# A delta rule's triangular inverse: the transposed inverse is kept and updated by products instead of being made by transposes

## The reference

```
g = jnp.cumsum(g, axis=-1)
decay = jnp.exp(jnp.where(tri_incl, g[..., :, None] - g[..., None, :], -jnp.inf))
k_beta = k * beta[..., None]
lower = jnp.where(tri_strict, jnp.einsum('bhncd,bhnsd->bhncs', k_beta, k) * decay, 0.0)
rhs = jnp.concatenate([v * beta[..., None], k_beta * jnp.exp(g)[..., None]], axis=-1)
sol = lax.linalg.triangular_solve(lower, rhs, left_side=True, lower=True, unit_diagonal=True)
...
v_new = ui - jnp.einsum('bhck,bhkv->bhcv', wi, state)
o = jnp.einsum('bhck,bhkv->bhcv', qd, state) + jnp.einsum('bhcs,bhsv->bhcv', qki, v_new)
state = state * jnp.exp(gl)[..., None, None] + jnp.einsum('bhck,bhcv->bhkv', kt, v_new)
```

## Time and profile before

| | us |
|---|---|
| median of 3 runs | 2580.62 |
| lowest and highest run | 2569.69, 2582.98 |
| span of the profiled execution | 2578.2 |
| TensorE busy in it | 2375.5 |
| VectorE busy in it | 1323.9 |
| ScalarE busy in it | 788.4 |
| GpSimd busy in it | 494.4 |

### The profile page before, as it was taken

One profiled execution on the slowest core, in us unless ns is written; L12 is line 12 of the kernel. 1 busy time (PEld: TensorE's weight loads), 2 busy tenths in 40 slices (PEclk: granted clock), 3 DMA queues, 4 the chain that ended last, 5 costly groups with the idle time before them and its releaser, 6 DMA issues.

```text
span 2578.2 us, 33292 instructions
## 1 busy us (share of the span) xinstructions
PE 2375.5 (92%) x13498; PEld 1918.1 (74%) x13498; DVE 1323.9 (51%) x1688; ACT 788.4 (31%) x1106; POOL 494.4 (19%) x350
## 2 busy tenths in 40 slices
PE   6867699999989999999999998999997987999997
PEld 5745577777877777788888876888885665888885
DVE  3799755664654243454445336444425675444423
ACT  4213322221542321333223224223223353233221
POOL 0799333313031332010000002000002013000001
PEclk8978898899989999999999997999997987999998
DMA  3221111111210111242223321222321101222321
GB/s 137 68 82 49 49 38 38 38 42 46 74 34 25 35 41 58 70 155 90 98 98 102 101 100 66 83 97 98 114 92 55 58 25 66 82 96 93 118 90 44
DMA packets 54899, 189.64 MB, mean 74 GB/s; under 512 B 6144, under 2 KB 6400, under 8 KB 54784
## 3 DMA queue, kind: packets, MB, share of 16 engines
q1 hardware_dynamic: 51904, 182.75, 20.9%
q10 hardware_dynamic: 2880, 5.24, 0.5%
HBM read 178.53 MB, written 9.44 MB: 73 GB/s over the span
## 4 chain that ended last, share of the span: by engine, by line
PE 75%; DVE 13%; issue 9%; ACT 1%; DMA 1%; SPq 0%; POOL 0%; DVEq 0%; ACTq 0%; POOLq 0%
PE pg L571 61%; PE pC L755 3%; DVE sacc L1606 2%; DVE cacc L1496 2%; PE pB L746 2%; PE pB L745 1%; PE pB L602 1%; DVE w_lo L1453 1%; DVE x L1932 1%; PE pC L609 1%; DVE a_lo L1478 1%; PE pB L609 1%; PE pC L746 1%; DVE hb L1928 1%; ACT w_hi L1027 1%
## 5 line engine op out<-in xcount | busy, mean ns | idle before, releaser
L571 PE MATMUL pg<-a_hi,w_hi 128*128 128x512 f32 x1904 | 780.4, 410 | 72.6 <-DVE a_lo L1478 36.9
L571 PE MATMUL pg<-a_hi,w_lo 128*128 128x512 f32 x1904 | 774.4, 407 | 0.0
L571 PE MATMUL pg<-a_lo,w_hi 128*128 128x512 f32 x1904 | 770.0, 404 | 0.0
L1453 DVE TENSOR_TENSOR w_lo<-w_raw,w_hi 128x1024 fp32r<-128x1024 f32 (+3 forms) x299 | 394.4, 1319 | 436.7 <-ACT w_hi L1027 436.7
L1027 ACT ACTIVATE w_hi<-w_raw 128x1024 fp32r<-128x1024 f32 (+3 forms) x299 | 329.7, 1103 | 700.4 <-PE pg L571 675.5
L571 PEld LDWEIGHTS pg<-a_hi,w_hi 128*128 128x128 f32 x1904 | 371.6, 195 | 168.1 <-issue 31.6
L571 PEld LDWEIGHTS pg<-a_hi,w_lo 128*128 128x128 f32 x1904 | 372.3, 196 | 80.4 <-issue 1.2
L571 PEld LDWEIGHTS pg<-a_lo,w_hi 128*128 128x128 f32 x1904 | 372.4, 196 | 75.2 <-issue 0.7
L2077 POOL TENSOR_TENSOR acc<-acc,sq 128x512 f32<-128x512 f32 x64 | 94.4, 1474 | 1382.1 <-ACT sq L1044 1381.2
L571 PE MATMUL pg<-h_hi,w_hi 128*128 128x512 f32 x528 | 208.0, 394 | 0.0
L571 PE MATMUL pg<-h_hi,w_lo 128*128 128x512 f32 x528 | 207.0, 392 | 0.0
(11 more groups left out here) (330 smaller groups left out, 2685.0 us busy)
## 6 DMA issues: line engine op xcount, KB each, us to landing
w_raw<-in_w_gu SPq DMA_DIRECT2D x132, 512.0 KB, 3.2
w_raw<-in_w_in SPq DMA_DIRECT2D x74, 512.0 KB, 3.2
w_raw<-in_w_dn SPq DMA_DIRECT2D x48, 704.0 KB, 4.1
spill_g<-tmp ACTq DMA_DIRECT2D x16, 256.0 KB, 2.0
w_raw<-in_w_co SPq DMA_DIRECT2D x8, 512.0 KB, 3.8
w_raw<-in_w_do SPq DMA_DIRECT2D x8, 512.0 KB, 3.6
w_raw<-in_w_wo SPq DMA_DIRECT2D x8, 512.0 KB, 3.9
w_raw<-in_w_pg SPq DMA_DIRECT2D x8, 512.0 KB, 7.5
```

The lines of the kernel that those rows point to most:

```text
L571: ins = pe.matmul(dst, w_of(w, n % 2, k), b(k), start=first and q == 0, stop=last and q == len(todo) - 1)
L1453: dve.tensor_tensor(w_lo[:, n % 2, 0:c], w_raw[:, n % 4, 0:c], w_hi[:, n % 2, 0:c].bitcast(F32), ALU.subtract).then_inc(S("w_lo"), 1)
```

## The change

The transposes of the running inverse are gone. The transposed inverse `tb` is updated at each level, as `ub` is: TensorE multiplies `yb` with `tb` into `ctr` right behind the second product, and VectorE takes that from `tb`. At level 5 only the 8 halves that are used later are made, and the half set of transposes after `yf` goes too. `turned` is removed: level 0's transposes are all matmuls against `id64`. The semaphores `tr` and `tcp` become `ty` and `t_upd`. On VectorE the update of `tb` stands behind the update of `ub`, where the copy stood ahead of it.

```diff
-            def turned(dst, src, s):
-
-                if s == halves[0]:
-                    return pe.transpose(dst, src, id64[s, :])
-                return pe.matmul(dst, src, id64[s, :], start=True, stop=True)
-
             def small(dst, lhs, rhs):
 
                 for j in range(J):
                     for s in halves:
-                        if rhs is None:
-                            ins = turned(dst[s, j, :], lhs[s, j, :], s)
-                        else:
-                            ins = pe.matmul(dst[s, j, :], lhs[s, j, :], rhs[s, j, :], start=True, stop=True)
+                        ins = pe.matmul(dst[s, j, :], lhs[s, j, :], id64[s, :] if rhs is None else rhs[s, j, :],
+                                        start=True, stop=True)
                 return ins
...
                     small(c0, ls[:, lv % 2], ub).then_inc(S("y"), 1)
-                    if lv > 1:
-                        small(ctr, ub, None).then_inc(S("tr"), 1)
                     gap(R, 2 * lv + 1)
                     pe.wait_ge(S("ycp"), LEVELS * R + lv)
-                    wait(pe, "tcp", (LEVELS - 1) * R + lv - 1)
+                    wait(pe, "t_upd", (LEVELS - 1) * R + lv - 1)
                     small(c1, tb, yb).then_inc(S("uy"), 1)
+                    if lv < LEVELS - 1:
+                        small(ctr, yb, tb).then_inc(S("ty"), 1)
+                    else:
+                        for j in range(J):
+                            b = halves[0] if j < HH else halves[1]
+                            ins = pe.matmul(ctr[b, j, :], yb[b, j, :], tb[b, j, :], start=True, stop=True)
+                        ins.then_inc(S("ty"), 1)
                     gap(R, 2 * lv + 2)
...
-                for j in range(J):
-                    b = lo if j < HH else hi
-                    ins = turned(ctr[b, j, :], en[b, j, b], b)
-                ins.then_inc(S("tr"), 1)
                 gap(R, 13)
                 pe.wait_ge(S("ycp"), LEVELS * (R + 1))
-                pe.wait_ge(S("tcp"), (LEVELS - 1) * (R + 1))
+                pe.wait_ge(S("t_upd"), (LEVELS - 1) * (R + 1))
...
                 for lv in range(1, LEVELS):
-                    if lv > 1:
-                        dve.wait_ge(S("tr"), (LEVELS - 1) * R + lv - 1)
-                        dve.tensor_copy(tb[:], ctr).then_inc(S("tcp"), 1)
                     gap(R, 2 * lv + 1)
...
+                    dve.wait_ge(S("ty"), (LEVELS - 1) * R + lv)
+                    if lv < LEVELS - 1:
+                        dve.tensor_tensor(tb[:], tb[:], ctr, ALU.subtract).then_inc(S("t_upd"), 1)
+                    else:
+                        dve.tensor_tensor(tb[lo_, 0:HH], tb[lo_, 0:HH], ctr[lo_, 0:HH], ALU.subtract)
+                        dve.tensor_tensor(tb[hi_, HH:J], tb[hi_, HH:J], ctr[hi_, HH:J], ALU.subtract)\
+                            .then_inc(S("t_upd"), 1)
...
-                dve.wait_ge(S("tr"), (LEVELS - 1) * (R + 1))
-                dve.tensor_copy(tb[lo_, 0:HH], ctr[lo_, 0:HH])
-                dve.tensor_copy(tb[hi_, HH:J], ctr[hi_, HH:J]).then_inc(S("tcp"), 1)
+                dve.wait_ge(S("yf"), R + 1)
```

## The result

The change makes the kernel faster: 2438.1 us median (2435.96 to 2442.74) against 2579.72 us for the kernel before in the same comparison, a ratio of 0.9459 with a 95% interval of [0.9438, 0.9479]. The forecast was 2451, its range 2440 to 2492; the measured median lies 2 us under the low end. The profiled execution has a span of 2441.0 us, 137.2 less than before, where the sum forecast 129.3 less.

A forecast was written before the change was run, and what follows sets the result against it. TensorE, busy throughout the level loops, was taken as the bound: 353.2 less 8 x 27.5 saves 133.2 us, 1.5 and 2.4 come back, so 2578.2 - 129.3 + 2.4 = 2451.3 us; range 2440 to 2492.

The forecast's parts named there:

- The bound: TensorE, busy in all 353.23 us of the eight level loops, bounds the kernel; the rest moves up rigidly.
- The price of the sets: On TensorE, a full set of sixteen plain products takes 1.08 us where sixteen alternating transposes took 3.43.
- The cause: In the transpose sets, alternating pe.transpose with matmul is what is slow: 0.214 us each against 0.067 for plain products.
- rival 3: In the new sets, products keep the alternating sets' 0.26 us pace, 4.16 us a set; slower, 2619 us; chance 0.04.
- rival 4: In the sets, writing pB or reading ub is slow, not alternation; sets stay 3.43, time 2581 us; chance 0.03.
- The clock: In the level loops, 39.6 us lost to the half clock (and a few short waits) are given back in full.
- Rival 2: In the level loops, the clock isn't given back; 93.6 us goes, 3.9 comes back, 2491 us; chance 0.10.
- The waits: Second product's wait for yb hidden by filler, cost nothing; level 0 waits 0.3 us in five blocks, 1.5 in all.
- The tail: Behind the last second product, yf comes 0.3 us a block later, 2.4 in all; removing the half set gains nothing.
- VectorE's load: In a level of R=0 to 3, VectorE takes 3.5 to 4.9 us against TensorE's 5.49, taps at 0.70 to 0.76.

The follow-up runs named there:

- e2: Kernel before with each transpose set reordered: eight lower halves (pe.transpose) first, then eight upper (matmul), one switch a set; 2476.62 us, ratio 0.9593.
- e1: Kernel before with every transpose made a matmul against the identity, nothing else changed; 2448.64 us, ratio 0.9491.
- e3: Kernel after the change with level 0 alone alternating pe.transpose and matmul again; 2473.34 us, ratio 0.9585.
- e4: Kernel after the change with the product for ctr done three times over at levels 1 to 4; 2501.84 us, ratio 0.9693.
- e5: Kernel after the change with the four filler matmuls between the two products moved behind the products; 2459.29 us, ratio 0.9532.
- e6: Kernel after the change with VectorE's update of tb at the old copy's place, behind L1739 and the taps; 2447.54 us, ratio 0.9486.
- e7: Kernel after the change with 2 filler matmuls, not 4, behind the new products and the freed 10 in gaps 0, 1 and 14; 2437.12 us, ratio 0.9452.
- e10: Kernel after the change with 3 filler matmuls, not 4, behind the new products, the freed 5 in gaps 14 and 1; 2432.19 us, ratio 0.9413.
- e8: Kernel after the change with VectorE's update of tb cut into eight subtractions of 64 columns; 2446.3 us, ratio 0.9474.

## Why the prediction was right, and where it was off

**The bound** was read rightly. The level loops had no idle time, TensorE's work in them fell, and 136.3 of 137.2 us came from there. The rest of the kernel moved up rigidly.

**The price of the sets** was right: 1.08 was taken and 1.08 (level 0) and 1.03 (ctr) measured. The second product got cheaper as well, 0.98, which I had not counted: forecast 27.5 us a loop, measured 27.1. The loops came to 216.9 and not 221.5 (8 x 27.5 and the 1.5 of level 0). That is 4.6 us of the difference of 7.9 between 137.2 and 129.3.

**The cause** given, the alternation of two kinds of instruction, stands: e2 keeps the instructions and changes the order alone, and the set goes from 3.43 to 1.64 us. Rivals 3 and 4 fall with e1 and e2: uniform sets still write pB and read ub, and take 1.03. The page that speaks for rival 3 (the Trainium skill, Perfetto Trace Analysis, section "Transposes") wants a transpose for each transpose. With e2's numbers that is right for one alone on a half, 0.071 against 0.134 us, and wrong for a set in which matmuls must stand between them. The Trainium skill (TensorEngine Tiling (Array Packing), section "Key Properties") says that a change of tiling mode drains the engine; that section doesn't say so of transposes, and no run here shows whether such a drain is what takes the 0.13 us.

**The clock** was given back in full in the loops, as taken. The 39.6 us were an inference from rows at first; e3 shows it happen again when one alternating set returns (12.5 us in six falls), and e4 that long runs of small products aren't the cause. Rival 2 falls. What in an alternating set lowers the clock stays open.

**The waits.** yb: right; e5 gives the price without cover at 0.7 us for each of 40 levels, and the filler covers it. Level 0: 0.26 us in five blocks (R=1 to 3, 5 and 7), as forecast.

**The tail** was taken at +2.4 us and is +0.1, which is another 2.3 us. The part that I priced came, and more: yf starts 1.96 us behind the last second product and not 1.55 to 1.75, 2.9 us in all. But I had put the half set of transposes under the chain and its removal at nothing, and that was wrong: the chain behind yf got shorter, 2.8 us in all. Before, VectorE's two copies to tb waited for that half set and stood ahead of w_lo in its queue. In R=5, before:

```profile
884.48 0.42 DVE L1745 COPY tb<-pB 64x256 f32<-64x256 f32 x1 [2.20 <-PE pB L746]
```

and after:

```profile
779.27 0.96 PE L803 MATMUL pC<-en 64*64 64x64 f32 x16
782.15 1.23 DVE L1446 TENSOR_TENSOR w_lo<-w_raw,w_hi 128x1024 fp32r<-128x1024 f32 x1 [1.17 <-ACT w_hi L1020]
784.32 2.05 PE L817 MATMUL pA<-en,kb 128*128 128x128 f32 x16 [0.72 <-DVE en L1747]
```

From yf to w_lo it is 2.88 us where it was 3.46, and to the product with the keys 5.05 where it was 5.62. In R=0 to 3, where taps stand in the queue too, the chain is 0.1 to 0.2 us shorter. That the two errors nearly cancel is luck.

**VectorE's load** was wrong too, though it hardly showed in the time. I took a tap at 0.70 to 0.76 us, from a mean over all taps. Of those 120, GpSimd was idle during 107 and busy throughout 3; after the change it is 96 and 17, since the shorter loops bring the taps under GpSimd's work. In the loops after the change:

```profile
408.50 2.80 DVE L1489 SCALAR_TENSOR_TENSOR cpad<-cpad,vec 128x512 f32<-128x512 f32 x2
409.27 2.93 POOL L2116 TENSOR_TENSOR bv<-vtok,gat 128x512 f32<-128x512 f32 x2
411.22 2.06 DVE L1446 TENSOR_TENSOR w_lo<-w_raw,w_hi 128x1024 fp32r<-128x1024 f32 x1
...
419.20 2.07 DVE L1489 SCALAR_TENSOR_TENSOR cpad<-cpad,vec 128x512 f32<-128x512 f32 x3
```

With GpSimd at work two taps take 2.80 us, 1.4 each, and w_lo 2.06; with GpSimd idle three taps take 2.07, 0.69 each. So the level that begins here has 0.69 + 0.69 for ub and tb, 0.6 for L1739, 2.8 and 2.0, 6.8 us of VectorE, and not the 4.9 that I had at most, against 5.4 of TensorE. It is hidden, but for a wait of 0.3 us for ub in three blocks, because ub may come 1.1 us later than before and the next level makes up for it. The same mis-sized term is what broke my expectation of e6 and ate much of the gain of e7.
The Trainium skill (GPSIMD Engine Reference, section "Specifications") says that GpSimd shares its SBUF interfaces with VectorE and contends with VectorE instructions that have two SBUF inputs. The trace agrees: taps and w_lo, with two such inputs, are slower, and the updates of ub and tb, with one input in PSUM, stay at 0.68. That section gives no size; weighed, it would have pointed at the taps and w_lo, and their price has to come from rows with GpSimd at work.

The last 1.0 of the 7.9 us isn't in the blocks: it lies in the stretch between the fourth block and the fifth, 136.9 us from the tail of R=3 to level 0 of R=4 before and 135.9 after. Why is open; the runs after spread by 7 us. The median lies 13.2 us under the forecast of 2451.3: 7.9 are these, and 5.3 come from the runs' own spread, for I took the median at 2.4 above the profiled span, and it is 2.9 below it. The profiled execution is the slowest of the four after, at 2442.74.

## What to carry to other kernels

Look at the pitch of a set of small TensorE instructions, start to start, before asking what to do without. Here sixteen alternating transposes and matmuls cost three times what sixteen of one kind did, and the clock fell behind them; one line would have brought 132 of the 141 us. When the order of work on a second engine changes, price its instructions from the stretch they will stand in, with the neighbours that are busy there, and not from a mean over the kernel. A step that seems to lie under a chain has to be followed to the engine that waits for it: the half set's copies were on the chain. And the slack won on TensorE brought more only where filler could be moved to a place at which it still waited, as e10 does with five matmuls; taken further, in e7, it came back as waits and as half clock.

## What the runs showed of the hardware

- A switch between a float32 `pe.transpose` and a matmul, 64x64 on opposite halves, costs about 0.13 us at 2.4 GHz (3.43 us with fifteen switches against 1.64 with one, for the same sixteen instructions).
- The granted clock fell to 0.50 behind 3.4 us in which TensorE was never idle but took 0.21 us for each small operation; 3.9 us of matmuls at 0.061 each left it at 1.00 (e4). In e7 it fell behind a wait of 1.7 to 1.8 us of TensorE in two blocks, and not behind the like wait in two others.
- A float32 tap of 128x512 on VectorE with both large inputs in SBUF takes 0.69 us with GpSimd idle and, in the rows shown, 1.4 to 1.6 with GpSimd busy; a subtraction with one input in PSUM takes 0.68 either way.
- Eight subtractions of 64 columns take 1.12 us in place of one of 512 columns in 0.69 (e8), so each takes 0.13 us from start to start.
